# Last layer's tokens taken by parity, output projections and conditioning in another order

## What is computed

```python
for l in (0, 1):                                  # first_block
    mod = silu(c) @ w_ada[l] + b_ada[l]           # 6 x 1024 conditioning values, context alike
    u = (rmsnorm(x) * (1 + sc_a) + sh_a) @ w_in[l]
    mixed = [fourier_mix(u), attention_group(u), hgrn_group(u)]
    x = x + g_a * (concatenate(mixed) @ w_out[l])
    x = x + g_f * swiglu(rmsnorm(x) * (1 + sc_f) + sh_f, w_gate[l], w_up[l], w_down[l])
# the context tokens get the same in layer 0, and only serve as keys and scan input in layer 1
B_GROUPS = ((128, 1), (512, 4), (2048, 16))
for i in (0, 1):                                  # second_block, layers 2 and 3
    h = rmsnorm_2(x, norm_mix[i]) * (1 + sc1) + sh1
    y = windowed_gqa(h, ...) if i == 0 else dilated_attention(h, ...)
    x = x + g1 * y
    x = x + g2 * swiglu_2(rmsnorm_2(x, norm_ffn[i]) * (1 + sc2) + sh2, ...)
# dilated_attention: three groups of 8 query and 2 key heads; a query sees the keys of its own
# residue modulo the group's dilation (1, 4, 16) within half a window; the three results are
# weighted by a softmax over their log denominators, which is one softmax over all their keys
```

## Time and profile before

| | us |
|---|---|
| median of three runs | 2096.52 (2089.58 to 2099.05) |
| the profiled execution, its own time | 2095.84 |
| span of its instructions | 2093.7 |
| TensorE busy | 1806.5 (86%) |
| VectorE busy | 1337.9 (64%) |
| ScalarE busy | 833.9 (40%) |
| GpSimd busy | 59.9 (3%) |
| HBM read | 297.56 MB, 143 GB/s over the span |
| TensorE on the chain that ended last | 70% of the span |

### The profile page before, as it was taken

The page is one execution under the profiler, slowest core; times in us unless marked ns, Lnnn a source line. Parts: engine busy times, 40 slices in busy tenths (PEclk is TensorE's granted clock), DMA queues, the critical chain, the costliest instruction groups (busy, mean ns, idle before and its releaser), DMA issues.

```text
span 2093.7 us, 30849 instructions
## 1 busy us (share of the span) xinstructions
PE 1806.5 (86%) x12222; PEld 1626.0 (78%) x12222; DVE 1337.9 (64%) x2476; ACT 833.9 (40%) x1601; POOL 59.9 (3%) x133
## 2 busy tenths in 40 slices
PE   4799888889989998798677999877799989579997
PEld 2689667877877887697576998675799879569996
DVE  1436877458876566667675687757588874465554
ACT  2523742252311221435533444356444444445442
POOL 0000031000000000000020000000000000000000
PEclk8899887989999999898777999988899999799999
DMA  8463010145555564233214898631589845014653
GB/s 281 125 201 86 17 47 21 41 122 171 185 172 165 181 196 156 72 112 87 81 41 121 244 270 263 219 95 27 161 244 278 291 141 153 21 41 121 183 179 132
DMA packets 359118, 300.60 MB, mean 144 GB/s; under 512 B 8048, under 2 KB 333408, under 8 KB 358592
## 3 DMA queue, kind: packets, MB, share of 16 engines
q1 hardware_dynamic: 357584, 294.22, 46.0%
q0 software_dynamic: 1392, 4.42, 0.9%
HBM read 297.56 MB, written 1.05 MB: 143 GB/s over the span
## 4 chain that ended last, share of the span: by engine, by line
PE 70%; DVE 15%; ACT 6%; issue 5%; DMA 3%; SPq 0%; DVEq 0%; ACTq 0%; POOLq 0%
PE bank L842 67%; PE bank L856 3%; ACT whigh L1334 2%; DVE ACC L1778 2%; DVE wlow L1762 1%; DVE A L2184 1%; ACT PB L1504 1%; DVE A L1859 1%; DVE A L2061 1%; DVE HTL L1865 1%; DMA A<-in_w_ada 1%; DVE A L2170 1%; DMA raw<-in_w_up 1%; DMA AWH<-in_ada_w 1%; DMA X<-in_ctx 0%
## 5 line engine op out<-in xcount | busy, mean ns | idle before, releaser
L1762 DVE TENSOR_TENSOR wlow<-raw,whigh 128x2048 fp32r<-128x2048 f32 (+1 forms) x183 | 409.9, 2243 | 329.6 <-ACT whigh L1334 329.2
L1334 ACT ACTIVATE whigh<-raw 128x2048 fp32r<-128x2048 f32 (+1 forms) x183 | 343.1, 1877 | 566.7 <-PE bank L842 387.1
L842 PE MATMUL bank<-HTH,whigh 128*128 128x256 f32 (+1 forms) x1424 | 446.8, 314 | 12.5 <-DVE HTL L1865 12.5
L842 PE MATMUL bank<-HTL,whigh 128*128 128x256 f32 (+1 forms) x1424 | 442.1, 310 | 0.0
L842 PE MATMUL bank<-HTH,wlow 128*128 128x256 f32 (+1 forms) x1424 | 441.7, 310 | 0.0
L842 PE MATMUL bank<-whigh,HTH 128*128 128x256 f32 (+1 forms) x1008 | 296.6, 294 | 14.9 <-DVE HTL L1865 5.8
L842 PEld LDWEIGHTS bank<-HTH,whigh 128*128 128x128 f32 x1424 | 275.4, 193 | 26.2 <-issue 13.6
L842 PE MATMUL bank<-wlow,HTH 128*128 128x256 f32 (+1 forms) x1008 | 292.6, 290 | 0.0
L842 PE MATMUL bank<-whigh,HTL 128*128 128x256 f32 (+1 forms) x1008 | 292.2, 290 | 0.0
L842 PEld LDWEIGHTS bank<-HTH,wlow 128*128 128x128 f32 x1424 | 274.9, 193 | 13.6
L842 PEld LDWEIGHTS bank<-HTL,whigh 128*128 128x128 f32 x1424 | 275.4, 193 | 12.5
(11 more groups left out here) (216 smaller groups left out, 2243.9 us busy)
## 6 DMA issues: line engine op xcount, KB each, us to landing
raw<-in_ffn_w_in SPq DMA_DIRECT2D x88, 512.0 KB, 5.3
A<-in_ada_w SPq DMA_DIRECT2D x42, 1024.0 KB, 6.7
A<-in_w_ada SPq DMA_DIRECT2D x32, 1024.0 KB, 5.5
raw<-in_w_gate SPq DMA_DIRECT2D x44, 512.0 KB, 4.2
raw<-in_w_up SPq DMA_DIRECT2D x44, 512.0 KB, 5.8
raw<-in_ffn_w_out SPq DMA_DIRECT2D x20, 1024.0 KB, 5.0
raw<-in_w_in SPq DMA_DIRECT2D x18, 1024.0 KB, 6.1
raw<-in_w_down SPq DMA_DIRECT2D x18, 1024.0 KB, 5.2
```

The lines of the kernel that those rows point to most:

```text
L842: return nc.tensor.matmul(out, lhsT, rhs, start=start, stop=stop, skip_group_check=True)
L1334: nc.scalar.activation(parts(loads[n])[0], raw_slot(loads[n]), ACT.Copy).then_inc(*made("split_high", loads[n]))
L1762: V.tensor_tensor(low, raw_slot(loads[n]), as_float(high), ALU.subtract).then_inc(*made("split_low", loads[n]))
```

## The change

- Layer 3's tokens are taken by parity: its tile 0 holds the even tokens and tile 1 the odd ones (`tokens_of`). In the groups of dilation 4 and 16 a query then sees keys of its own tile only, so these groups have 128 keys instead of 256: `PIECES3` is 256, 128 and 128 columns, 512 a head. The input projection reads its left operand with a step of two, the attended values are written back with the same step, and from the output projection on tokens stand in their order. Layer 3 uses the same banks, buffers and loop order as the others; the distance table is stored accordingly.
- `gate_rows` of the mixing moves into the input projection, ahead of its last column group, in all layers, on TensorE and ScalarE.
- In layer 0 the output projection begins with the context tiles; in layer 1 with six of eight blocks for the first two column groups. The Fourier outputs and the turns of the read-out move into it, and VectorE's and ScalarE's operations follow that order.
- In the feed-forwards the conditioning matmuls run two blocks behind (`late(key, by=2)`), banks of the down projection are opened at a tile's first matmul, and VectorE drains a half ahead of the last chunk's conditioning sum and split. `ada_plan` gives layer 0's feed-forward 30 chunks for 35, layer 1's 20 for 17, layer 2's 20 for 18, on one place fewer.
- In the scan VectorE adds a read-out value before the next gate sum.

The core of the diff, with indents shortened:

```diff
--- before.py
+++ after.py
@@ -87,7 +87,13 @@
-    return np.ascontiguousarray(out.reshape(4, 2, P, N).transpose(2, 0, 1, 3))
+    order = np.concatenate([np.arange(0, N, 2), np.arange(1, N, 2)])
+    last = out[1:][:, order][:, :, order]
+    parts = [out[0].reshape(2, P, N).transpose(1, 0, 2).reshape(P, 2 * N)]
+    for t in range(2):
+        r = slice(P * t, P * t + P)
+        parts.append(np.concatenate([last[0, r], last[1, r, r], last[2, r, r]], 1))
+    return np.ascontiguousarray(np.stack(parts, 1))
@@ -96,8 +102,8 @@
-    wide = np.array(slopes(24)).reshape(GROUPS3, 8).T.reshape(-1)
-    return np.ascontiguousarray(np.broadcast_to(np.concatenate([slopes(16), wide]), (P, 40)).astype(np.float32))
+    wide = np.array(slopes(24)).reshape(GROUPS3, 8).T[:, [0, 0, 1, 2]].reshape(-1)
+    return np.ascontiguousarray(np.broadcast_to(np.concatenate([slopes(16), wide]), (P, 48)).astype(np.float32))
@@ -216,7 +222,7 @@
-    keys = [key for key in load_plan() if key[1] == l and key[0] in ("gu", "dn")][1:-1]
+    keys = [key for key in load_plan() if key[1] == l and key[0] in ("gu", "dn")][1:-2]
@@ -224,9 +230,9 @@
-give(feed_forward(0, 35))
+give(feed_forward(0, 30))
 ...
-give(feed_forward(1, 17))
+give(feed_forward(1, 20))
@@ -263,6 +269,23 @@
+def out_jobs(l):
+    n = len(out_loads(l))
+    if l:
+        return [(j, t) for j in range(n) for t in X_TILES]
+    return [(j, t) for tiles in (C_TILES, X_TILES) for j in range(n - 1) for t in tiles] + [(n - 1, t) for t in C_TILES + X_TILES]
+def last_job(l, j):
+    return [t for j2, t in out_jobs(l) if j2 == j][-1]
+def out_parts(l):
+    return ((1, C_TILES), (0, X_TILES)) if l == 0 else ((0, X_TILES),)
@@ -287,8 +310,13 @@
-def turned_banks(l):
-    return 3 if l == 3 else 2
+TURNED = 2
+PIECES3 = ((0, 256), (256, 128), (384, 128))
+def tokens_of(l, t):
+    return slice(t, N, 2) if l == 3 else slice(P * t, P * t + P)
@@ -891,13 +911,16 @@
-last_load = [None]
-def late(key):
-    if last_load[0]:
-        beside(*last_load[0])
-    last_load[0] = key
+held = []
+def late(key, by=1):
+    while len(held) >= by and held:
+        beside(*held.pop(0))
+        if key:
+            break
+    if key:
+        held.append(key)
@@ -925,9 +948,9 @@
-            h_ready(l, "mix", t)
+            h_ready(l, "mix", *(X_TILES if l == 3 else (t,)))
 ...
-        r = slice(P * t, P * t + P)
+        r = tokens_of(l, t)
@@ -937,6 +960,8 @@
+    if at == len(col_groups(l)) - 2:
+        gate_rows(l, "mix")
@@ -1017,25 +1042,25 @@
-    if n >= (1 if l == 3 else 2):
-        pe.wait_ge(*upto("probs", l, n - (1 if l == 3 else 2)))
+    if n >= 2:
+        pe.wait_ge(*upto("probs", l, n - 2))
 ...
-            for g in range(GROUPS3):
-                mm(ps[:, e, N * g:N * g + N], EYE[:, :], DISTR[:, 1 + g, t, :], g != 1, False)
-        for g in range(GROUPS3):
+            mm(ps[:, e, :], EYE[:, :], DISTR[:, 1 + t, :], True, False)
+        for g, (at, size) in enumerate(PIECES3):
+            keys = slice(0, N) if g == 0 else slice(P * t, P * t + P)
 ...
-                    last = mm(ps[:, e, N * g:N * g + N], q[r, x, 4 * g + p, P * t:P * t + P], k[r, y, 2 * g + p // 2, :],
+                    last = mm(ps[:, e, at:at + size], q[r, x, 4 * g + p, P * t:P * t + P], k[r, y, 2 * g + p // 2, keys],
 ...
-                mm(ps[:, e, :], EYE[:, :], DISTR[:, 0].rearrange("p t c -> p (t c)"), True, False)
+                mm(ps[:, e, :], EYE[:, :], DISTR[:, 0, :], True, False)
@@ -1062,17 +1087,18 @@
-    before = g - (1 if l == 3 else 2)
+    before = g - 2
 ...
-    nk = 512 * turned_banks(l) // w
+    nk = 512 * TURNED // w
 ...
-            left = [v[:, y, i % 2, P * (i // 2):P * (i // 2) + P] for y in range(2)]
+            group, tile = ((0, 0), (0, 1), (1, u["tiles"][0]), (2, u["tiles"][0]))[i]
+            left = [v[:, y, tile, P * group:P * group + P] for y in range(2)]
@@ -1084,12 +1110,10 @@
-    if l < 3 and n + 1 < len(units):
+    if n + 1 < len(units):
 ...
-    if l == 3 and n + 1 < len(units):
-        scores(n + 1)
@@ -1211,23 +1235,59 @@
-    for t in tiles_of(l, "ffn"):
-        pe.wait_ge(*upto("attended_low", l, t))
+    jobs, shape, entered, banks_of = out_jobs(l), out_loads(l), set(), {}
+    def enter(t):
+        if t in entered:
+            return
+        entered.add(t)
+        for t2 in X_TILES if l == 3 else (t,):
+            pe.wait_ge(*upto("attended_low", l, t2))
 ...
-            pe.wait_ge(*drained("m", l, t, 0))
-    if l < 2:
-        for g in range(2 if l == 0 else 1):
-            pe.wait_ge(*drained("ff", l, g))
-    for j, (nk, nc_) in enumerate(out_loads(l)):
+            pe.wait_ge(*drained("ff", l, t // 2))
+    def some(j, t, ks):
+        nk, nc_ = shape[j]
 ...
-        for t in tiles_of(l, "ffn"):
-            ps = open_bank("x1", l, j, t)
-            r = slice(P * t, P * t + P)
-            for k in range(nk):
-                last = mm3(ps[:, 0:nc_], (HTH[:, k, r], HTL[:, k, r]), (wh[:, k, :], wl[:, k, :]), k == 0, k == nk - 1)
+        if ks[0] == 0:
+            banks_of[j, t] = open_bank("x1", l, j, t)
+        ps = banks_of[j, t]
+        r = slice(P * t, P * t + P)
+        for k in ks:
+            last = mm3(ps[:, 0:nc_], (HTH[:, k, r], HTL[:, k, r]), (wh[:, k, :], wl[:, k, :]), k == 0, k == nk - 1)
+        if ks[-1] == nk - 1:
 ...
+    if l >= 2:
+        for j, t in jobs:
+            enter(t)
+            some(j, t, range(shape[j][0]))
+        return
+    if l == 0:
+        fourier_out(l, 1)
+        mixed_turns(l, C_TILES)
+    fourier_out(l, 0)
+    whole = [(j, t) for j, t in jobs if t in C_TILES and j < len(shape) - 1]
+    for j, t in whole:
+        enter(t)
+        pe.wait_ge(*drained("m", l, t, 0))
+        some(j, t, range(8))
+    begun = [(j, t) for j, t in jobs if l == 1 and j < 2]
+    for j, t in begun:
+        enter(t)
+        some(j, t, range(6))
+    mixed_turns(l, X_TILES)
+    for j, t in begun:
+        pe.wait_ge(*drained("m", l, t, 0))
+        some(j, t, range(6, 8))
+    for j, t in jobs:
+        if (j, t) not in whole + begun:
+            enter(t)
+            pe.wait_ge(*drained("m", l, t, 0))
+            some(j, t, range(8))
@@ -1273,6 +1333,8 @@
+                if c == 0:
+                    ps[t] = open_bank("x2", l, half, h, t)
@@ -1891,17 +1950,17 @@
-def project_out(l):
-    for j, (_, n) in enumerate(out_loads(l)):
-        for t in tiles_of(l, "ffn"):
-            i = cond_of_tile(t) if l < 2 else 0
-            dve.wait_ge(*drained("g", l, "mix", i, n * j // 512))
-            ps = take("x1", l, j, t)
-            link(V.tensor_tensor(ps[:, 0:n], ps[:, 0:n], grow[:, i, n * j:n * j + n], ALU.mult))
-            x = X[:, t, n * j:n * j + n]
-            V.tensor_tensor(x, ps[:, 0:n], x, ALU.add).then_inc(*made("drained_dve", "x1", l, j, t))
-        if j < len(out_loads(l)) - 1:
+def project_out(l, jobs):
+    for j, t in jobs:
+        n = out_loads(l)[j][1]
+        i = cond_of_tile(t) if l < 2 else 0
+        dve.wait_ge(*drained("g", l, "mix", i, n * j // 512))
+        ps = take("x1", l, j, t)
+        link(V.tensor_tensor(ps[:, 0:n], ps[:, 0:n], grow[:, i, n * j:n * j + n], ALU.mult))
+        x = X[:, t, n * j:n * j + n]
+        V.tensor_tensor(x, ps[:, 0:n], x, ALU.add).then_inc(*made("drained_dve", "x1", l, j, t))
+        if j < len(out_loads(l)) - 1 and t == last_job(l, j):
@@ -2220,10 +2279,10 @@
+    if n and steps[n - 1][3]:
+        take_read(n - 1)
 ...
-    if n and steps[n - 1][3]:
-        take_read(n - 1)
@@ -2244,6 +2303,15 @@
+    def drain(half, h):
+        for t in tiles_of(l, "ffn"):
+            i = cond_of_tile(t) if l < 2 else 0
+            dve.wait_ge(*drained("g", l, "ffn", i, h))
+            ps = take("x2", l, half, h, t)
+            link(V.tensor_tensor(ps[:, :], ps[:, :], grow[:, i, 512 * h:512 * h + 512], ALU.mult))
+            x = X[:, t, 512 * h:512 * h + 512]
+            V.tensor_tensor(x, ps[:, :], x, ALU.add).then_inc(*made("drained_dve", "x2", l, half, h, t))
@@ -2260,16 +2328,11 @@
+                if c == len(down_chunks(l, half)) - 1:
+                    drain(half, h)
 ...
-            for t in tiles_of(l, "ffn"):
-                i = cond_of_tile(t) if l < 2 else 0
-                dve.wait_ge(*drained("g", l, "ffn", i, h))
-                ps = take("x2", l, half, h, t)
-                link(V.tensor_tensor(ps[:, :], ps[:, :], grow[:, i, 512 * h:512 * h + 512], ALU.mult))
-                x = X[:, t, 512 * h:512 * h + 512]
-                V.tensor_tensor(x, ps[:, :], x, ALU.add).then_inc(*made("drained_dve", "x2", l, half, h, t))
```

114 lines of the change are left out of this document (51 added, 63 removed).

## The result

| | before | changed |
|---|---|---|
| median of three runs, us | 2096.52 | 2056.79 (2055.41 to 2060.70) |
| the profiled execution, its own time | 2095.84 | 2060.70 |
| span of its instructions | 2093.7 | 2058.5 |
| ratio, 95% interval | | 0.983 [0.980, 0.985] |

The change made the kernel 39.7 us faster by the medians, 35.2 by the spans. The forecast was 2032, 64.5 us faster: the direction is right, the time lies 0.8 us beyond the range. For the experiments the kernel before was run again beside each group, with medians of 2091.28 to 2093.54; their ratios are to those.

What follows compares the result with a forecast made beforehand. The prediction saw a chain of stages where TensorE mostly streams, with time to win where it stands still. Terms summed to -63.9 on a 2093.7 span: 2029.8, plus 2.1 and 0.7, forecast 2032 us, range 2008 to 2056.

Steps and rivals of the forecast that it cites:

- Attention of layer 3: Layer 3's attention takes layer 2's shape, VectorE bounding at 4.2 us a unit: stage 41.5 us, -36.
- Feed-forward of layer 0: Three edits remove TensorE's waits and the lower clock behind them, and five chunks leave: -33 us.
- residual additions: Layer 0's feed-forward: TensorE's 11.9 us of waits behind the down projection's residual addition go.
- the two-block lateness: Layer 0's feed-forward: conditioning matmuls two weight blocks behind instead of one remove 3.6 us of waits on conditioning sums.
- the doubled places: Layer 0's feed-forward: with 30 chunks on 31 places none holds two, removing 3.8 us behind the conditioning bank's drain.
- Feed-forwards of layers 1 and 2: Three and two more chunks there, with 3 us of stalls in each layer: +5 us together, bounds -1 and +21.
- so there is just room: Layers 1 and 2's feed-forwards: demand of 288 GB/s with the added chunks stays under 295 GB/s at most.
- rival 1: DMA becomes the bound in layers 1 and 2: 13 us more for chunks, 7 for lower clock; 2052 us, chance 0.14.
- my sign of being wrong: Layers 1 and 2: the forecast is wrong if landings stop TensorE there.
- Output projections: Layers 0 and 1: projections start earlier, less turns, drains and moved gate rows: -2.8 and -2.9 us.
- Gate rows of layers 2 and 3, start of layer 3: Gate rows move into the projection, layer 2 +2.3 us; layer 3's first products need both tiles, +5.5 with its gate rows.
- rival 4: Layer 3's projection: 432 strided weight loads each stand uncovered, +85 us, 2117 us, slower; chance 0.03.

Runs made afterwards that it cites:

- before_plan: Kernel before with only the change's numbers of conditioning chunks (30, 20, 20 on 31 places each); 2104.9 us, ratio 1.006.
- twelve_23: spread_gates with 12 and 23 conditioning chunks beside the feed-forwards of layers 1 and 2; 2036.4 us, one execution.
- half_chunks: Changed kernel, but the 40 conditioning chunks beside layers 1 and 2's feed-forwards load half their bytes, that half used twice; 2032.8 us, one execution.
- plan_back: Changed kernel with conditioning chunks on their old places (35, 17, 18 beside the feed-forwards of layers 0, 1, 2); 2062.9 us, ratio 0.986.
- plan_and_one_block: plan_back with conditioning products one block behind everywhere instead of two; 2065.5 us, ratio 0.988.
- gates_back: Changed kernel with the mixing's gate rows behind attention and scan again in all four layers; 2042.9 us, ratio 0.978.
- spread_2: spread with 8, 31, 8, 16, 17 chunks and the gate rows of layers 2 and 3 behind the attention; 2029.9 us, ratio 0.971.
- spread: Changed kernel, ScalarE's drain ahead of the split; 8, 31, 6, 17, 18 chunks (layer 0 scan, feed-forward; layer 1 scan; feed-forwards 1, 2); 2030.9 us.
- spread_gates: spread and gates_back together, against the changed kernel; 2023.55 us, ratio 0.967.

## Why the prediction was right and wrong

**Attention of layer 3**: right, mechanism and size. The stage fell by 35.0 us to 42.5 for the 36 and 41.5 given, the seven intervals from 1784.74 to 1813.05 are 4.04 each for 4.2, and VectorE bounds them, as forecast. The one us missing is in the filling and emptying, 42.5 - 28.3 = 14.2 for 11.8. Some 1.5 us are lost behind it. TensorE now stands idle for 2.98 us where the gate rows had stood, so the output projection comes no sooner after the attention than before, and its first matmuls run at the lower clock: 0.53 from 1830.0 to 1833.4 us, where the kernel before had 1.00.

**Feed-forward of layer 0**: the sum is right (-33.7 for -33), the shares are not. I gave the residual additions 11.9 us and most of the 13.6 at the lower clock, the two-block lateness 3.6, the doubled places 3.8. In runs the new number of chunks alone is 20.3 (before_plan); what is left for the additions is then 13.4 (415.2 to 401.8), while taking them out of the changed kernel costs 22.1; and the lateness is nothing with 30 chunks and 10 us of harm with 35. So the shares depend on the order in which the edits are made: without the additions' edit the new kernel waits 17.4 us for them, the old one 11.5 with the same number of chunks. Three fifths of this stage's gain could be had by one number.

**Feed-forwards of layers 1 and 2**: here the prediction failed. I gave the five chunks **+5** in all and they cost 27.2 (13.0, and 17.0 less 2.85); these 22 us are most of the 24.8 by which the median missed the forecast. The failed step is "so there is just room". It divided bytes by TensorE's time in the gate and up phase alone and set 288 GB/s (its own terms give 289) against 295, a rate that came from 274 at a share of 0.93 by assuming that a whole phase could run at a share of 1. Single windows of 20 us do get there: the kernel before moved 287 GB/s at 0.99 from 1570 to 1590 us, and 313 at 0.93 in a window of its down projection. Whole phases don't. Layer 1's gate and up phase and then its down projection, before and changed:

```profile
1150.90:1289.40 138.50, 135.73 (x1116) 135.07 (x1117) 104.16 (x151) 60.18 (x90) 0.00 (x0) 0.99 0.87 259
1289.40:1352.30 62.90, 62.90 (x290) 52.02 (x289) 49.64 (x68) 24.14 (x28) 0.00 (x0) 1.00 0.68 230
```

```profile
1115.40:1257.60 142.20, 138.65 (x1124) 137.81 (x1125) 109.55 (x167) 60.02 (x92) 0.00 (x0) 0.97 0.87 260
1257.60:1329.80 72.20, 66.82 (x294) 54.54 (x293) 54.28 (x76) 24.91 (x33) 0.00 (x0) 0.95 0.68 229
```

The added chunks did not raise the rate, they lengthened the phases. The gate and up phases move 259 and 263 GB/s before, 260 and 261 after, and 266 with 23 chunks (twelve_23). They grew by only 3.7 and 5.8 us (138.5 to 142.2, in layer 2 137.1 to 142.9). The down projections grew by 9.3 and 8.4 (62.9 to 72.2, 63.2 to 71.6), two thirds of the loss, and for them the sum had no term: there a block takes TensorE only 24 x 0.227 + 0.2 = 5.65 us, hence 1.727 MB / 5.65 = 306 GB/s asked for. Why whole phases stay near 260 was not tried. SP issues a load only when its place is free, and in layer 1's feed-forward it waits 77.9 us for the places of chunks, for 47.6 before (but 69.0 in half_chunks, where TensorE lost nothing); a rate of the engines and a shortage of places would both fit. The Trainium skill's DMA: Bandwidth & Descriptors, section Specifications, has about 358 GB/s for one core; no gate and up phase here moved more than 267, and by that page these chunks would have been free, so here the measurement decides.

The size was off as well as the case: rival 1 had this mechanism, with 13 + 7 on top of my 5, so 25 us, close to the 27 measured. It had 0.14 where the share of 0.93 was itself a sign of the limit; its "against", that no wait of TensorE ended with a landing, was no argument: in the changed kernel none does either. For the same reason my sign of being wrong, landings that stop TensorE, never showed. The waits carry the name of the instruction that stands behind the late split, the drain or the low half.

**Output projections**: layer 0 can't be called right. From the start to its feed-forward it takes 2.8 us less for -2.8 and some -1 of the scan, but 2 us of that are a faster start. The eight experiments from plan_back to plan_and_one_block have the changed kernel's code up to this point, and they reach it after 439.9 to 449.1 us, for 446.0 before: one execution can't show a term of this size. What was priced for the projection's start came true: it went from 15.9 us behind the scan to some 6 (378.13 us for the first product). But the gate rows cost more than their 3.73 us, as shown above: gates_back gives 9.8 back at the start and takes 6.3 later. Layer 1: forecast -2.9, measured +1.0. Counted from its first scores TensorE starts the projection 4.7 us sooner (133.4 for 138.1), but takes 6.0 more from there to the feed-forward (43.8 for 37.8), since the norm comes no sooner:

```profile
1107.56 1.76 PE L876 MATMUL bank<-ident,A 128*128 128x128 f32 x7 [9.54 <-DVE A L1899]
```

```profile
1095.72 2.29 DVE L1821 TENSOR_TENSOR wlow<-raw,whigh 128x2048 fp32r<-128x2048 f32 x1 [4.72 <-ACT whigh L1391]
```

VectorE's last residual additions stand behind splits of the feed-forward's first blocks, which are still landing. I had priced what starts the projection, not what ends it. That this is the cause was read from the trace and not tried, and this stage differs by some 4 us from one execution to another, as said under spread_2.

**Gate rows of layers 2 and 3, start of layer 3**: +1.5 for +2.3, and 2.85 + 1.3 = +4.2 for +5.5. The step-of-two operand cost nothing: layer 3's weight loads from 1735 to 1784 us, to be set beside the earlier trace rows:

```profile
L862 PEld LDWEIGHTS bank<-whigh,HTH 128*128 128x128 f32 x99 | 19.4, 196 | 2.8 <-DVE KHL L2028 2.8
```

196 ns, as before; rival 4 is out. By the Trainium skill's Advanced Engine Details and Errata, section SBUF Cachelines, two fp32 elements on a line suffice, and this row agrees.

## What to carry to other kernels

Hold what a stage asks of DMA against the rate that whole phases of it have moved, not against a window's rate divided by its share: here the gate and up phases moved 259 and 263 GB/s before and 260 and 261 after, though single windows reached 287. And take the demand phase by phase, because the phase with the shortest time per block decides. When work is spread over places, what counts is where the slack is: four chunks cost a scan at most some 2 us, five chunks and three places that held two cost 20 beside layer 0's feed-forward, and chunks beyond 17 or 18 cost 3 to 7 us each in the feed-forwards of layers 1 and 2. And a small job moved to make one place earlier has to be priced at its new place with the banks and queues there. In this kernel the gate rows were moved out of waits of some 3 us; putting them back went with medians 7 us lower (spread against spread_gates) and 14 (gates_back), both with overlapping intervals, while in layer 0's projection alone they take some 7.

## What was not expected of the hardware

A large loss from late weights appears as no wait on a landing on the engine that loses the time: 7 to 12 us on `modc`, `ACC` or `wlow` in a stage, depending on what stands next in the queue, and some 4 to 6 us as a lower clock behind them (0.97 and 0.96 for 0.99 over 214 us). ScalarE's splits do show the landings, but they showed them before the change as well: in layer 1's feed-forward they wait 79 us for them before and 98 after. The sum is read from the stage's length alone.
